# Three mixtures of experts in a fused two-block kernel: barriers after routing removed, rank products merged, weights and gathers asked for earlier

## The reference, cut to what matters

```
p1 = softmax(tokens @ w1 + b1);  p_grp, grp = top_k(p1, 1)
lg2 = (tokens @ w2 + b2) of that group;  top_val, top_idx = top_k(lg2, 2)
gate = p_grp * softmax(top_val);  expert = grp * per_group + top_idx
y = sum over the 2 experts of gate * ((silu(x @ w_gate[e]) * (x @ w_up[e])) @ w_down[e])
x = layer_norm(alpha * x + g2 * y)
```

## Time and profile before

| what | us |
|---|---|
| median of 3 runs (2935.01 to 2935.58) | 2935.51 |
| the profiled execution's own time | 2930.33 |
| its span | 2928.7 |
| mixture 1: rank products to last context product | 445.7 to 877.1 |
| mixture 2: rank products to last combined tile | 1196.7 to 1932.3 |
| mixture 3: rank products to the end | 2335.8 to 2928.7 |

### The profile page before, as it was taken

The page is one execution under the profiler, slowest core; times in us unless marked ns, Lnnn a source line. Parts: engine busy times, 40 slices in busy tenths (PEclk is TensorE's granted clock), DMA queues, the critical chain, the costliest instruction groups (busy, mean ns, idle before and its releaser), DMA issues.

```text
span 2928.7 us, 34027 instructions
## 1 busy us (share of the span) xinstructions
PE 2476.4 (85%) x11132; PEld 1300.0 (44%) x11132; DVE 839.4 (29%) x1467; ACT 463.5 (16%) x894; POOL 275.4 (9%) x412
## 2 busy tenths in 40 slices
PE   8998694999879989569999998399999749997771
PEld 3333352444454545334445444155675424444440
DVE  1125731000047865300000000361375510000004
ACT  2113411100030020110101110121453101000000
POOL 2212402000010000200000000100001010000001
PEclk9998996999989999679999999699999869999995
DMA  9865138998751120599999989520002079999993
GB/s 342 327 259 186 8 102 307 421 420 307 255 186 58 58 88 5 212 406 424 418 416 412 414 360 415 206 88 29 15 16 64 0 319 423 426 400 421 421 407 124
DMA packets 150509, 744.39 MB, mean 254 GB/s; under 512 B 13648, under 2 KB 15360, under 8 KB 101264
## 3 DMA queue, kind: packets, MB, share of 16 engines
q1 hardware_dynamic: 101648, 595.61, 51.0%
q0 software_dynamic: 34512, 110.87, 10.8%
q10 hardware_dynamic: 14256, 36.71, 3.4%
HBM read 664.26 MB, written 79.46 MB: 254 GB/s over the span
## 4 chain that ended last, share of the span: by engine, by line
PE 71%; DMA 15%; DVE 7%; issue 3%; DVEq 1%; ACT 1%; POOL 1%; ACTq 1%; POOLq 0%; SPq 0%; PEldq 0%
PE ps L684 14%; PE ps L235 13%; PE ps L765 8%; DMA x_feat<-in_e_down 7%; PE ps L707 7%; PE ps L373 7%; PE ps L790 6%; PE ps L245 3%; PE ps L1221 2%; DMA arena<-expert_outputs,slots_i 2%; DMA arena<-expert_rows 2%; PE ps L1244 1%; PE ps L1232 1%; PE ps L675 1%; PE ps L362 1%
## 5 line engine op out<-in xcount | busy, mean ns | idle before, releaser
L684 PE MATMUL ps<-w_ring,arena 128*128 128x512 f32 x960 | 424.2, 595 | 5.2 <-issue 4.3
L235 PE MATMUL ps<-x_feat,w_ring 128*128 128x512 f32 (+1 forms) x992 | 381.6, 545 | 1.6 <-issue 1.0
L684 PEld LDWEIGHTS ps<-w_ring,arena 128*128 128x128 f32 x960 | 178.2, 190 | 229.5 <-issue 227.7
L235 PEld LDWEIGHTS ps<-x_feat,w_ring 128*128 128x128 f32 x992 | 187.4, 190 | 192.9 <-issue 185.0
L707 PE MATMUL ps<-w_ring,arena 128*128 128x512 f32 x480 | 213.8, 599 | 8.5 <-DMA w_ring<-in_w_down 6.9
L373 PE MATMUL ps<-w_ring,x_feat 128*128 128x512 f32 x448 | 196.5, 598 | 13.7 <-ACTq L146 12.1
L765 PE MATMUL ps<-arena 128*64 128x256 f32 x1472 | 175.8, 393 | 37.5 <-DMA arena<-in_e_gate 33.7
L790 PE MATMUL ps<-x_feat,arena 128*64 128x512 f32 x784 | 183.3, 610 | 23.5 <-DMA x_feat<-in_e_down 22.5
L765 PE MATMUL ps<-w_ring,arena 128*64 128x256 f32 x1568 | 186.6, 392 | 19.3 <-DMA w_ring<-in_e_up 19.3
L774 DVE TENSOR_TENSOR arena<-arena,ps 128x256 f32<-128x256 f32 x49 | 20.6, 421 | 540.1 <-PE ps L765 540.1
L765 PEld LDWEIGHTS ps<-arena 128*64 128x64 f32 x1472 | 105.8, 141 | 121.8 <-DMA arena<-in_e_gate 48.6
(11 more groups left out here) (286 smaller groups left out, 2425.7 us busy)
## 6 DMA issues: line engine op xcount, KB each, us to landing
w_ring<-in_e_up SPq DMA_DIRECT2D x61, 2048.0 KB, 12.5
x_feat<-in_e_down SPq DMA_DIRECT2D x43, 2048.0 KB, 12.3
arena<-in_e_gate SPq DMA_DIRECT2D x41, 2048.0 KB, 12.2
w_ring<-in_ada_w SPq DMA_DIRECT2D x24, 2048.0 KB, 13.5
w_ring<-in_e_gate SPq DMA_DIRECT2D x22, 2048.0 KB, 12.9
w_ring<-in_e_down SPq DMA_DIRECT2D x20, 2048.0 KB, 9.8
w_ring<-in_w_up SPq DMA_DIRECT2D x15, 2048.0 KB, 11.9
w_ring<-in_w_gate SPq DMA_DIRECT2D x11, 2048.0 KB, 12.1
```

Of the source, the lines that this page charges most:

```text
L235: mm = nc.tensor.matmul((at or pair)(j)[:, t0:t1], w[:, k, c0:c0 + P], x_feat[:, k, t0:t1], start=k == 0, stop=k == KT - 1)
L684: mm = nc.tensor.matmul(bank(2 + part), blk_feat[:, s, k, :], w[:, k, :], start=k == 0, stop=k == KT - 1)
```

## The change

- The barriers route1 to route3 go. Each engine waits for what it needs: TensorE and GpSimd's visits for `table`, ScalarE for `table` and the completed scatter; ScalarE and VectorE for the last modulation stores before the buffers that those occupy.
- VectorE computes the running sum of `both` over the tiles; the ranks and totals become four products.
- The slots are finished and signalled (`slots`) before the tables; the scatter waits for `slots`.
- SyncE loads gate and up of the first small visit on `table`; those of the first large visit still wait for the scatter.
- The last rows are asked for before the scatter, when the last tile of the projection is normalised. In mixture 2 the columns are awaited, and 1 added, before the visits.
- The gather no longer waits between tiles; two semaphores by parity tell when a tile is there. It starts when ScalarE has left the visits.
- Mixtures 1 and 3: VectorE scales the residual by alpha after the scatter, and the combine is two multiply-adds; in mixture 3 the g2 row is multiplied in as the visits' outputs are evicted (for a small visit two instructions instead of one). Mixture 2: ScalarE scales the first rows.
- In turns without a visit, one drain stands for two on ScalarE and VectorE.

The diff, cut to its core:

```diff
@@ moe_router_pe
-            for t in range(m.T):
-                for s in range(t + 1):
-                    nc.tensor.matmul(bank(1)[:, t * m.E:(t + 1) * m.E], ones if s < t else tri_strict,
-                                     chosen[:, s, :], start=s == 0, stop=s == t)
-            for s in range(m.T):
-                mm = nc.tensor.matmul(bank(2)[:, 0:m.E], ones, chosen[:, s, :], start=s == 0, stop=s == m.T - 1)
+            upto = moe_arrays(m)["tail"]
+            n = m.T * m.E
+            nc.tensor.matmul(bank(1)[:, 0:m.E], tri_strict, chosen[:, 0, :], start=True, stop=True)
+            nc.tensor.matmul(bank(1)[:, m.E:n], tri_strict, chosen[:, 1:, :].rearrange("p t e -> p (t e)"),
+                             start=True, stop=False)
+            nc.tensor.matmul(bank(1)[:, m.E:n], ones, upto[:, 0:m.T - 1, :].rearrange("p t e -> p (t e)"),
+                             start=False, stop=True)
+            mm = nc.tensor.matmul(bank(2)[:, 0:m.E], ones, upto[:, m.T - 1, :], start=True, stop=True)
@@ moe_router_dve
-            v.tensor_tensor(a["both"], a["all1"], a["all2"], ALU.add).then_inc(summed[f"{name}.ranks_in"], 1)
+            then(v.tensor_tensor(a["both"], a["all1"], a["all2"], ALU.add))
+            upto = a["tail"]
+            v.tensor_copy(upto[:, 0], a["both"][:, 0])
+            for t in range(1, T):
+                dve.drain()
+                ins = v.tensor_tensor(upto[:, t], upto[:, t - 1], a["both"][:, t], ALU.add)
+            ins.then_inc(summed[f"{name}.ranks_in"], 1)
...
+            dve.drain()
+            v.tensor_reduce(a["sl"][:, 0], a["all1"], axis=AX.X, op=ALU.add)
+            v.tensor_reduce(a["sl"][:, 1], a["all2"], axis=AX.X, op=ALU.add)
+            dve.drain()
+            v.tensor_copy(slots_i[:, :, 0:T], a["sl"])
+            dve.drain().then_inc(summed[f"{name}.slots"], 1)
@@ moe_scatter
-            pool.wait_ge(*count(f"{name}.table", 1))
+            pool.wait_ge(*count(f"{name}.slots", 1))
@@ Doubles.take_outputs
+                if self.gate_row is not None:
+                    return nc.vector.tensor_tensor(blk_out[:, s, :], ps[:, 2560:3584], self.gate_row, ALU.mult)
@@ moe_sp
-            sp.wait_ge(*count(f"{name}.scattered", 32 * m.T))
...
-            for kind in kinds:
+            for n, kind in enumerate(kinds):
+                if n == 1:
+                    sp.wait_ge(*count(f"{name}.scattered", 32 * m.T))
                 for slot, (part, w) in enumerate((("gate", gate), ("up", up))):
@@ moe_blocks_act
+            act.wait_ge(*count(f"{name}.table", 1))
             n_used = [kind.used(act) for kind in kinds]
             most = most_visits(act, m)
             first = [kind.first_row(act) for kind in kinds]
+            act.wait_ge(*count(f"{name}.scattered", 32 * m.T))
...
+            for n in ada[-ADA_BUFFERS:]:
+                act.wait_ge(*ada_sent(n))
             with act.Fori(0, m.turns) as turn:
@@ moe_gather_pool
-                    ).then_inc(summed[f"{name}.gathered"], 16)
-                pool.wait_ge(*count(f"{name}.gathered", 32 * (t + 1)))
-                pool.sem_inc(summed[f"{name}.both_rows"], 1)
+                    ).then_inc(summed[f"{name}.gathered{t % 2}"], 16)
@@ new functions
+        def residual_ahead_dve(dve, name, m, alpha):
+            dve.wait_ge(*count(f"{name}.scattered", 32 * m.T))
+            for t in range(m.T):
+                nc.vector.tensor_scalar(x_tok[:, t, :], x_tok[:, t, :], alpha, None, ALU.mult)
+
+        def first_rows_act(act, name, t):
+            act.wait_ge(*both_rows(name, t))
+            y1 = picked[:, 2 * (t % 2), :]
+            nc.scalar.activation(y1, y1, ACT.Copy, scale=gate_w[:, 0, t:t + 1]).then_inc(summed[f"{name}.scaled"], 1)
@@ moe_combine_dve (mixtures 1 and 3)
-                nc.vector.tensor_scalar(y1, y1, gate_w[:, 0, t:t + 1], None, ALU.mult)
-                dve.drain()
-                nc.vector.scalar_tensor_tensor(y1, y2, gate_w[:, 1, t:t + 1], y1, ALU.mult, ALU.add)
...
+                nc.vector.scalar_tensor_tensor(x, y1, gate_w[:, 0, t:t + 1], x, ALU.mult, ALU.add)
+                dve.drain()
+                nc.vector.scalar_tensor_tensor(x, y2, gate_w[:, 1, t:t + 1], x, ALU.mult, ALU.add).then_inc(
+                    summed[f"{name}.picked_free"], 1)
@@ gpsimd, mixture 2
+            pool.wait_ge(*count("out2.h_here", TA))
+            load_last_rows(d["ln"][6], d["ln"][7], mod(0, 0, 5), mod(0, 1, 5))
             moe_scatter(pool, "moe2", MOE2, h_tok, ADA_ROUTE2)
-            stage(pool, "pool", "route2")
-            load_last_rows(d["ln"][6], d["ln"][7], mod(0, 0, 5), mod(0, 1, 5))
             load_columns_of_mods(col3, 1)
-            moe_blocks_pool(pool, "moe2", MOE2)
             loaded()
             nc.gpsimd.tensor_scalar(col3[:, :, 0, :], col3[:, :, 0, :], 1.0, None, ALU.add)
             pool.drain().then_inc(summed["moe2.cols_here"], 1)
-            pool.wait_ge(*count("moe2.visited", 2))
+            moe_blocks_pool(pool, "moe2", MOE2)
+            pool.wait_ge(*count("moe2.rows_in", 1))
             moe_gather_pool(pool, "moe2", MOE2)
```

More of the change, by code:

```diff
@@ L452, in route_counts @@
             return {"t.ready": 2 * T, "t.read": 2 * T, "logits": 1, "exps": 2, "exps_done": 2, "ranks_in": 1,
-                    "ranks": 1, "table": 1, "scattered": 32 * T, "gathered": 32 * T, "both_rows": T,
-                    "picked_free": T, "var": T, "root": T, "combined": T, "visited": 2, "cols_here": 1}
+                    "ranks": 1, "slots": 1, "table": 1, "scattered": 32 * T, "gathered0": 16 * T, "gathered1": 16 * T,
+                    "picked_free": T, "var": T, "root": T, "combined": T, "rows_in": 1, "outputs_done": 1, "cols_here": 1}
         def visit_counts(n):
@@ L795, in take_outputs @@
             def take_outputs(self, s):
+                if self.gate_row is not None:
+                    for half in range(2):
+                        at = slice(self.H * half, self.H * (half + 1))
+                        ins = nc.vector.tensor_tensor(half_out[at, s, :], bank(7)[at, :],
+                                                      self.gate_row[at, 512 * half:512 * (half + 1)], ALU.mult)
+                    return ins
                 return nc.vector.tensor_copy(half_out[:, s, :], bank(7))
@@ L891, in down @@
                 kinds[n].down(s, 1).then_inc(summed[at(n, "free")], 1)
+            pe.wait_ge(*count(f"{name}.table", 1))
             n_used = [kind.used(pe) for kind in kinds]
@@ L1025, in outputs @@
                 kinds[n].take_outputs(s).then_inc(summed[at(n, "y_copied")], 1)
+            for n in ada[-ADA_BUFFERS:]:
+                dve.wait_ge(*ada_sent(n))
             n_used = [kind.used(dve) for kind in kinds]
@@ L1060, in at @@
                 return f"{name}.{kinds[n].kind}.{part}"
+            pool.wait_ge(*count(f"{name}.table", 1))
             n_used = [kind.used(pool) for kind in kinds]
@@ L1101, in moe_combine_dve, with moe_combine_gated_dve @@
+        def moe_combine_gated_dve(dve, name, m, alpha, gate, g, b):
+            for t in range(m.T):
+                dve.wait_ge(*count(f"{name}.scaled", t + 1))
+                y1, y2 = picked[:, 2 * (t % 2), :], picked[:, 2 * (t % 2) + 1, :]
                 nc.vector.scalar_tensor_tensor(y1, y2, gate_w[:, 1, t:t + 1], y1, ALU.mult, ALU.add)
                 dve.drain()
-                if gate is not None:
-                    nc.vector.tensor_tensor(y1, y1, gate(t), ALU.mult)
-                    dve.drain()
+                nc.vector.tensor_tensor(y1, y1, gate(t), ALU.mult)
+                dve.drain()
@@ L1379, in build @@
         new_sems("x3", "ready", "read")
+        new_sems("moe2", "scaled")
+        MOE3.gate_row = last_rows[2]
         new_sems("in3", "ready", "read")
```

89 lines of the change are left out of this document (48 added, 41 removed).

## The result

The changed kernel takes **2892.35 us** (median of four runs, 2891.74 to 2895.11) against 2935.26 of the kernel before beside it (2930.33 to 2935.58): a ratio of 0.986, interval 0.9842 to 0.9877. Forecast were 2896.5, and 2891 for the profiled execution. That one took 2891.74 around a span of 2890.0, where the kernel before had 2930.33 around 2928.7: 38.6 us less, of a forecast 39.

What follows compares the result with a forecast made beforehand. Rounds fill TensorE and DMA, so gains must come from mixtures' heads and tails, where the chain leaves TensorE. Heads 3, 10.5, 2 plus tails 5.2, 10.5, 7.9 make 39 us: 2891 profiled, 2896.5 median; range 2877 to 2915.

Steps and rivals of the forecast that it cites:

- Ranks and slots: Heads: four products for the ranks gain 2, 7 and 3.6 us; slots before tables gain 1.4, 4.2 and 4.1.
- Stores beside weights: Heads: indirect stores, slowed by small visits' gate and up loading alongside, end at about 479, 1239 and 2369.5.
- The stores keep a third: Heads: engines share by piece, 4 KB against 8, so indirect stores get 133 of 400 GB/s.
- Rival A: Heads: stores are hardly hurt and end 5 us sooner in each; 2881, down to 2876; chance 0.18.
- The early start is spent: Heads: stores start 3.5, 11 and 7.7 us earlier but end about 479, 1239, 2369.5, against 472, 1240, 2367.4.
- Both loads at 390 GB/s in any order end no later: Heads: a bound, indirect stores and weight loads together finish no later than about 479, 1239 and 2369.5.
- Barrier: Heads: rows wait for stores alone, asked for at 485.7, 1246 and 2370, against 485.75, 1253.8 and 2371.0.
- Last rows: Heads: two, four and three 512 KB broadcasts no longer share engines with row loads; sent and hidden before routing.
- Landings: Heads: rows land at 500, 1260 and 2384.7; gains 3, 10.5 and 1 us, 1 more in mixture 3.
- Tails: Last store to last normalised tile: gains of 5.2, 10.5 and 7.9 us in mixtures 1, 2 and 3.
- rival E: Mixture 2's end: 6 us stay at POOL's first gather after an addition; 5.2 more, 2901.7; chance 0.10.
- The sum: Whole kernel: all gains add to 39 us, 2930.3 to 2891 in the profiled execution, 2896.5 in the median.

## Why the prediction was right, point by point

**Ranks and slots: right.** 1.5, 7.9 and 2.9 us by the run that undid the ranks, for 2, 7 and 3.6. The stores were to start 3.5, 11 and 7.7 earlier and did by 3.0, 10.7 and 6.9 (the first counted from L570, which stood 0.35 earlier). What this leaves for the slots ahead of the tables, 1.5, 2.8 and 4.0 for 1.4, 4.2 and 4.1, is a difference: no run undid that part alone.

**Stores beside weights: right in mechanism and size.** "The stores keep a third": q0 moved 131 to 141 GB/s with about as many packets as q1 (144 to 154, and 144 to 157, in 4 us). With the modulation stores behind them they ended at 479.9, 1231.9 and 2341.5. Set back by the 8.5 and 28.25 that each mixture begins earlier, these are 479.9, 1240.4 and 2369.7, for 479, 1239 and 2369.5. Rival A falls with it. "The early start is spent" was true, but I priced the alternative too low. "Both loads at 390 GB/s in any order end no later" was meant for the stores and the small pair together, and the rows were to follow the last of them. The order decides what the rows wait for, and undoing it gave 28 us, not the 15 of rival A.

**Barrier: right.** Rows asked for at 485.4, 1245.7 and 2369.9 by the same reckoning, for 485.7, 1246 and 2370. Putting it back cost 18 us. In mixtures 1 and 2 the rows were then asked for 9.5 and 9.9 us later after the first store, more than the prediction's 5.31 + 2.35, but landed faster (in mixture 1 in 11.50 us for 15.33), and 6.5 and 6.4 were left; in mixture 3 I had only the 1.0 between 2371.0 and 2370 and not that the rows now stand ahead of the large pair.

**Last rows: a term that was not there.** Undone alone they moved nothing. The 1 us that mixture 3 was to gain at the second large gate was there (0.93), but with the broadcasts back behind the scatter, in a head 3 us longer, TensorE does not wait for that gate either, so nothing shows that they were its cause.

**Landings: 500 and 1260 right, with some luck in what followed, the third mis-sized.** 501.1 and 1261.2 came, each 1.1 late. The heads still gave 2.7 and 11.0 for 3 and 10.5, because the small gate's 32 products behind them took 4.47 and 4.18 us instead of 5.48 and 5.77: in mixture 1 the granted clock was 1.00 from 505, four us after the landing, where before it was still 0.76 from 507 to 511, as late after its own. The prediction has nothing of this. As for the third, in mixture 3 the rows took 11.65 us, not 14.6, and head 3 gave 4.4 for 2. The likely cause is the one just named: they were asked for 0.2 us ahead of the large pair (2342.00 and 2342.18). By the DMA records the small visit's rows moved from 2342.64 to 2343.94, and the first data of the large gate at 2343.53; the large visit's rows moved from 2346.39 to 2352.53, beside the pair, so for these it is not shown.

**Tails: right in sum, each within 1.1.** In mixture 1 TensorE's pace was 7.8, not 8.0, and the gain 5.7. In mixture 2 rival E is out: 7.24 us before the gather, as the 6.58 that stand ahead of the addition where it was put back, so this is the loop's end, and 16.2 instead of 8.4 from store to gather with the addition put back. "0.8 us after POOL's loop" came as said (0.81 behind its last branch), and the store to gather time fell from 13.96 to 8.36, 5.6 for 5.2. What filled the 6.00 the prediction did not see: by the trace nearly all of it is the drain behind the addition, with 5.44, and in the two runs that put a computing instruction and a drain right ahead of a gather the drain takes 2.0 to 7.7. In mixture 3 I had taken 0.65 for the last eviction's second half, but from the eviction's start to the gather it was 1.2 more (10.40 for 9.18), and I missed a gap of 0.48 inside the first tile: 6.8 for 7.9.

**The sum** was right also because errors offset each other: +2.4 in head 3 and about -2.4 given back between. That is luck.

## What to carry to other kernels

A load that "hides beside" another on the same DMA engines was not free here, since everything waited for the other. The weights were not needed before 503, some 42 us after they were asked for, and took two thirds of the bandwidth (285 to 295 of 423 to 430 GB/s) from the stores; a wait of one line in front of them was worth 28 us, two thirds of what the whole change brought. Rank what is asked for by who needs it next, and look at the size of the pieces: these two queues got 144 packets each in the 4 us from 1221, and the one with pieces of 4 KB moved 131 GB/s, the one with 8 KB 295. And where a head is bound by bytes, an earlier first product says little: with the rows first it came 27.3 us after the first store in mixture 1, for 38.7 with the weights held back alone, and the head was only 3.2 shorter. Measure to the point where the engine no longer waits.

## What the hardware showed that I had not expected

**GpSimd's drain is not of one size.** 2.0, 4.6, 5.4, 5.9 and 7.7 us behind a computing instruction, in the rows above, which make gaps of 2.7, 5.3, 6.0, 6.6 and 8.3 us ahead of the next indirect DMA. The timeline shows only the gap, as "issue"; the drain is found by its source line.

**TensorE comes out of the heads at half clock.** In the changed kernel the first expert products start at 503.15, 1254.7 and 2355.7, and the granted clock is 0.50 up to 504.8, 1255.7 and 2358.2 and 1.00 behind. In the run with the rows first it is 0.50 from 470 to 490, where TensorE is busy for 10.4 of the 20 us, and the first 32 products of a small visit take 6.27 us; at a granted 1.00, at 515.99, they take 3.67. One stretch of its table:

```profile
486.00:490.00 4.00, 4.00 (x22) 2.23 (x20) 0.00 (x0) 0.00 (x0) 0.00 (x0) 0.52 1.06 276
```

Its 276 GB/s, with engines over-full, falls together with the column loads of the modulations, as in the earlier trace rows: they are asked for from 482 on, and from 486 to 492 the rate is 240 to 310 GB/s, with 422 on both sides. In mixture 2 it is 330 and 293 from 1224 to 1232, and in mixture 3, which has no such loads in its head, 428 and 444 in the like stretch from 2320. That they are the cause is argued from this; moving them was not tried.

**Identical code varies ahead of mixture 1.** In the eleven executions profiled of kernels that are equal up to there, the first store stood between 454.5 and 461.0 us. This is about as much as the profiled execution of the kernel before lay below its median (2930.3 against 2935.3), and it is why lengths of heads and tails tell more here than single times.
